# A mixture of experts on one core: the last expert's block moved into the counted loop, and the output matrices asked for by SyncE

## What is computed

```python
def moe_ffn(h, router_w, router_b, w_in, w_out):      # t: 512 tokens x 1024
    ...
    top_p, top_e = lax.top_k(in_group, TOP_K)         # 2 of 16 experts for each token
    ...
    for e in range(N_EXPERTS):
        gu = t @ w_in[e]                              # 1024 x 768
        act = jax.nn.silu(gu[:, :D_EXPERT]) * gu[:, D_EXPERT:]
        y = y + gates[:, e:e + 1] * (act @ w_out[e])  # 384 x 1024
```

## Time and profile before

| | |
|---|---|
| median of three runs | 2024.51 us (2021.44 to 2024.57) |
| the profiled execution, its own time | 2025.37 us |
| its span, first to last instruction | 2023.0 us |
| PE matmul busy, share of the span | 1597.4 us, 79% |
| DVE busy | 931.6 us, 46% |
| ACT busy | 696.4 us, 34% |
| POOL busy | 148.4 us, 7% |
| mean granted TensorE clock | 0.865 of full speed |
| bytes moved | 279.68 MB |

### The profile page before, as it was taken

The page is one execution under the profiler, slowest core; times in us unless marked ns, Lnnn a source line. Parts: engine busy times, 40 slices in busy tenths (PEclk is TensorE's granted clock), DMA queues, the critical chain, the costliest instruction groups (busy, mean ns, idle before and its releaser), DMA issues. The chain is left out here.

```text
span 2023.0 us, 19236 instructions
## 1 busy us (share of the span) xinstructions
PE 1597.4 (79%) x7495; PEld 1287.3 (64%) x7495; DVE 931.6 (46%) x1327; ACT 696.4 (34%) x1080; POOL 148.4 (7%) x162
## 2 busy tenths in 40 slices
PE   6992799376689793999973898879688793999973
PEld 5881767365577472878852787768577472878852
DVE  3224456534362525666624324552263526666623
ACT  3211234312251413555522325131251413655521
POOL 0001000100000001111010002140000001111110
PEclk8995558657899896999996899989899896999996
DMA  3324000001232026799962241213232016799963
GB/s 135 101 64 69 2 1 1 2 1 63 86 125 86 0 84 235 286 356 356 354 223 83 94 156 63 84 42 104 86 125 86 0 42 243 285 357 360 349 215 125
DMA packets 110604, 279.68 MB, mean 138 GB/s; under 512 B 40865, under 2 KB 43570, under 8 KB 105906
## 3 DMA queue, kind: packets, MB, share of 16 engines
q1 hardware_dynamic: 94962, 207.13, 29.9%
q10 hardware_dynamic: 5760, 54.53, 7.2%
q0 software_dynamic: 9792, 16.80, 2.2%
HBM read 273.11 MB, written 24.12 MB: 147 GB/s over the span
## 5 line engine op out<-in xcount | busy, mean ns | idle before, releaser
L185 DVE TENSOR_TENSOR w_lo<-w_stage,w_hi 128x2048 fp32r<-128x2048 f32 (+2 forms) x74 | 171.4, 2326 | 414.1 <-ACT w_hi L175 414.1
L175 ACT ACTIVATE w_hi<-w_stage 128x2048 fp32r<-128x2048 f32 (+2 forms) x74 | 135.9, 1847 | 473.0 <-PE bank L214 374.2
L2102 PE MATMUL bank<-e_wo,e_actT 128*128 128x512 f32 x408 | 181.0, 593 | 3.0 <-ACT e_actT L2162 3.0
L1996 DVE TENSOR_TENSOR e_wi_lo<-e_wi,w_hi 128x1536 fp32r<-128x1536 f32 x64 | 112.5, 1757 | 57.2 <-ACT w_hi L1992 57.2
L2102 PEld LDWEIGHTS bank<-e_wo,e_actT 128*128 128x128 f32 x408 | 76.7, 190 | 84.9 <-issue 83.1
L1996 DVE TENSOR_TENSOR e_wi_lo<-e_wi,w_lo 128x1536 fp32r<-128x1536 f32 x64 | 112.5, 1758 | 17.9 <-ACT w_lo L1992 17.9
L1992 ACT ACTIVATE w_hi<-e_wi 128x1536 fp32r<-128x1536 f32 x64 | 95.2, 1490 | 49.8 <-PE bank L2091 38.0
L1992 ACT ACTIVATE w_lo<-e_wi 128x1536 fp32r<-128x1536 f32 x64 | 95.0, 1484 | 18.2 <-PE bank L2091 17.1
L2090 PE MATMUL bank<-e_wi_lo,e_hx_hi 128*128 128x384 f32 x272 | 92.9, 342 | 0.0
L2091 PE MATMUL bank<-e_wi_lo,e_hx_hi 128*128 128x384 f32 x272 | 92.5, 340 | 0.0
L2218 DVE TENSOR_TENSOR e_hx_lo<-bank,e_hx_hi 128x512 fp32r<-128x512 f32 x68 | 43.8, 685 | 86.3 <-ACT e_hx_hi L2155 86.3
(11 more groups left out here) (470 smaller groups left out, 3908.7 us busy)
## 6 DMA issues: line engine op xcount, KB each, us to landing
e_wi<-in_moe_w_in SPq DMA_DIRECT2D x136, 768.0 KB, 6.0
e_wo<-in_moe_w_out ACTq DMA_DIRECT2D x32, 1536.0 KB, 9.0
w_stage<-in_x_wkv SPq DMA_DIRECT2D x16, 1024.0 KB, 5.1
w_stage<-in_sg_w_in SPq DMA_DIRECT2D x16, 1024.0 KB, 5.3
w_stage<-in_hyb_w_in SPq DMA_DIRECT2D x10, 1024.0 KB, 5.1
w_stage<-in_x_wq SPq DMA_DIRECT2D x8, 1024.0 KB, 6.2
w_stage<-in_x_wo SPq DMA_DIRECT2D x8, 1024.0 KB, 5.9
w_stage<-in_sg_w_out SPq DMA_DIRECT2D x8, 1024.0 KB, 5.0
```

The costliest lines, as they stand in the source:

```text
L175: act.activation(self.w_hi[h][:, :, :cols], self.stage[h][:, :, :cols], ACT.Copy)\
L185: dve.tensor_tensor(self.w_lo[h][:, :, :cols], self.stage[h][:, :, :cols], self.w_hi[h][:, :, :cols], ALU.subtract).then_inc(self.lo_done[ ...
L1996: dve.tensor_tensor(self.lo[q][:, :, :], self.raw[q][:, :, :], self.hi[q], ALU.subtract).then_inc(self.wi_los[q], 1)
L2102: ins = pe.matmul(y_ps[n][:, :], auT[:, f, :], wo[j][:, f, n * GC:(n + 1) * GC], start=f == 0, stop=f == CO - 1)
```

## The change

Three things change. The diff is cut to them; the rest of it moves semaphore counts by one and makes `slots` and `meta` one column larger.

1. Straight-line code now ends with block 14 (`L = NE - 1`). The loop starts with block 15, so it makes one pass more. The first entry of `meta` is expert 15, and its count is one more. In the loop a pass uses buffer 1, and turns the tokens of the next block behind its own products.
2. The output matrices of experts 2 to 14 are asked for by SP, behind the input matrix of the same expert, and wait for `wo_used`. ACT asks for none in straight-line code but the one of expert 1.
3. The tokens of block 1 are turned behind the products of block 0, no longer ahead of them.

```diff
-MAXB = (2 * S) // P + NE - 1
+MAXB = (2 * S) // P + NE
...
+                dve.memset(ebf[:, 0:1], float(NE - 1))
+                link(dve.tensor_scalar(ebf[:, OV + 1:OV + 2], cum[0:1, NE - 1:NE], 1.0, None, ALU.add))
...
             def _(sp):
-                for e in range(2, NE):
+                for e in range(2, L):
                     w.load_in(sp, e, e)
-                with sp.Fori(0, extra(sp)) as i:
+                    sp.wait_ge(wo_used, e - 1)
+                    w.load_out(sp, e, wo[e % 2])
+                with sp.Fori(0, rest(sp)) as i:
...
-                for b in range(2):
-                    pe.wait_ge(w.hx_in[b], 16)
+                def turn_tokens_of(b):
+                    pe.wait_ge(w.hx_in[b % 2], 16 * (b // 2 + 1))
                     if b:
                         pe.wait_ge(h_lo, b)
-                    turn_tokens(b)
-                for b in range(NE):
+                    turn_tokens(b % 2)
+
+                turn_tokens_of(0)
+                for b in range(L):
...
                     if b:
                         outputs_of(b - 1)
+                    else:
+                        turn_tokens_of(1)
...
-                outputs_of(NE - 1)
-                with pe.Fori(0, extra(pe)) as i:
+                outputs_of(L - 1)
+                with pe.Fori(0, rest(pe)) as i:
+                    pe.wait_ge(h_lo, i + NE)
+                    for q in range(CI):
+                        pe.wait_ge(w.wi_los[q], i + NE)
+                        product(1, q)
                     pe.wait_ge(w.hx_in[0], i * 16 + 16 * (NE // 2 + 1))
                     turn_tokens(0)
...
                     finish(b % 2)
-                    if b + 2 < NE:
-                        w.load_out(act, b + 2, wo[b % 2])
...
+                with act.Fori(0, rest(act)) as i:
                     e = expert(act, i)
-                    act.dma_start(wo[0][:, :, :], ...).then_inc(w.wo_in[0], 16)
+                    act.dma_start(wo[1][:, :, :], ...).then_inc(w.wo_in[1], 16)
+                    for q in range(CI):
+                        act.wait_ge(wi_used[q], i + L)
+                        act.wait_ge(w.wi_in[q], i * 16 + 16 * NE)
+                        act.activation(w.hi[q], w.raw[q][:, :, :], ACT.Copy).then_inc(w.wi_his[q], 1)
...
+                    silu()
                     act.wait_ge(h_turned, i + NE + 1)
-                    keep_tokens(0)
...
+                    keep_tokens(1)
```

More of the change, by code:

```diff
@@ L2060, in _ @@
                     scatter(b, b % 2, slots[:, 1, b:b + 1])
[L2061 to L2065, removed]
+                with pool.Fori(0, rest(pool)) as i:
+                    pool.tensor_copy(ix[:, 0:1], slots[:, 0, bass.ds(i + NE, 1)]).then_inc(ix_set, 1)
+                    pool.wait_ge(h_turned, i + NE)
+                    pool.wait_ge(ix_set, i * 2 + 1)
                     pool.sem_inc(passed, 1)
                     w.gather(pool, None, 0, ix[:, 0:1], h_dram)
-                    pool.wait_ge(y_act, i + NE + 1)
-                    pool.wait_ge(y_dve, i + NE + 1)
+                    pool.tensor_copy(ix[:, 1:2], slots[:, 1, bass.ds(i + L, 1)]).then_inc(ix_set, 1)
+                    pool.wait_ge(ix_set, i * 2 + 2)
+                    pool.wait_ge(y_act, i + NE)
+                    pool.wait_ge(y_dve, i + NE)
                     pool.sem_inc(passed, 1)
[L2071 to L2075, removed]
+                    scatter(None, 1, ix[:, 1:2])
+                    pool.wait_ge(w.hx_in[0], i * 16 + 16 * (NE // 2 + 1))
+                    pool.wait_ge(stored[1], i * 16 + 16 * (NE // 2))
+                    pool.sem_inc(passed, 1)
+                pool.wait_ge(stored[0], 16 * (NE // 2))
             @block.tensor
@@ L2134, in _ @@
                     turn_activations()
[L2135 to L2136 removed]
+                outputs_of(L - 1)
[4 more added lines that the diff above has]
+                        product(1, q)
                     pe.wait_ge(w.hx_in[0], i * 16 + 16 * (NE // 2 + 1))
                     turn_tokens(0)
[L2139 to L2143, removed]
[L2144 to L2149 removed]
+                    pe.wait_ge(multiplied, i + NE)
+                    turn_activations()
+                    pe.wait_ge(aT_out, i + NE)
+                    pe.wait_ge(w.wo_in[1], i * 16 + 16 * (NE // 2))
+                    pe.wait_ge(y_act, i + L)
+                    pe.wait_ge(y_dve, i + L)
+                    outputs(1)
             @block.scalar
@@ L2232, in finish_of @@
                     finish(b % 2)
[L2234 to L2238, removed]
+                dve.wait_ge(h_hi, 1)
+                keep_tokens(0)
+                for b in range(L):
+                    if b + 1 < L:
                         for q in range(CI - 1):
@@ L2251, in _ @@
                         keep_tokens(b % 2)
-                finish_of(NE - 1)
-                with dve.Fori(0, extra(dve)) as i:
-                    dve.wait_ge(h_hi, i + NE + 1)
[L2255 to L2263, removed]
+                finish_of(L - 1)
+                with dve.Fori(0, rest(dve)) as i:
+                    for q in range(CI):
+                        dve.wait_ge(w.wi_his[q], i + NE)
+                        dve.tensor_tensor(w.lo[q][:, :, :], w.raw[q][:, :, :], w.hi[q], ALU.subtract).then_inc(w.wi_los[q], 1)
+                    dve.wait_ge(silued, i + NE)
+                    multiply()
+                    dve.wait_ge(h_hi, i + NE + 1)
+                    keep_tokens(1)
+                    dve.wait_ge(wo_used, i + NE)
+                    dve.wait_ge(stored[1], i * 16 + 16 * (NE // 2 - 1))
+                    finish(1)
 def moe_combine(m, layer, w, wgt, y_dram):
```

61 lines of the change are left out of this document (30 added, 31 removed).

## The result

The changed kernel takes 2051.12 us (median of four runs, 2041.65 to 2054.64), the one before 2022.97 us in the same comparison. The ratio is 1.0138, with a 95% interval of 1.0096 to 1.0179: slower by 28 us (19 to 36 by the interval), as forecast (2054). But two of the three terms behind that number were badly wrong, and it was luck that their errors cancelled. The profiled execution took 2049.9 us against 2025.37 before.

A forecast was written before the change was run, and what follows sets the result against it. PE was taken to set the pace mid-stage, with transfers having little to spare. Start 6.2, steady part 7.2 and end 1.1 made 14.5 us a layer, 29 for two layers, so about 2054 us, ranging from 2041 to 2068.

The forecast's parts named there:

- the four stretches in the table: One layer cut at start, blocks to 14, end, and hand-over to `moe_combine`; forecast +6.2, +7.2, +1.1 and 0 us.
- The start: Block 1's tokens turned behind block 0's products: PE idle about 4.8 us, then half clock, +6.2 us a layer.
- the bounds 3.9 and 6.2: Start of the stage: +3.9 us a layer as the low end, +6.2 if the idle gap loses the clock.
- The steady part: Blocks 2 to 13: PE waits 1.2 us in every second block, six waits, +7.2 us a layer.
- The burst: SP's requests after PE's outputs: output matrix first, then four input quarters, 1536 + 4 x 768 KB.
- the chain through DVE to `multiply`: Steady part: quarter 2's high and low parts precede DVE's `multiply`, which PE needs to turn the activations.
- the slack of 11.5 us: Steady part: quarter 2 may land 11.5 us after the request before PE has to wait.
- the eight loads of `moe_combine`: Steady part: 4096 KB burst used as measure, giving 11.4 us, or 12.7 with gather and scatter.
- The end: Block 15 in the loop: two passes of about 24.6 us, +1.1 us a layer, bounds -3.5 and +3.1.
- two are 49.2, against 48.97 for block 15 in the row and one pass as it was: End of the stage: two loop passes after the change replace straight-line block 15 plus one pass before.
- The burst runs at the stage's own rate: Rival for the steady part: burst at 357 GB/s, +13.8 us a layer there, 2067 us in all; chance 0.12.
- That the change doesn't do what it says: Loop at the end: more or fewer passes than two; given no chance of its own.

The follow-up runs named there:

- alone: Kernel before with only the later turning of block 1's tokens (part 3) added: 2032.21 us, ratio 1.0060.
- beside the loop's part: Changed kernel with ACT asking for the output matrices as before, 1992.85 us, against the same with the later turning undone too, 1977.83 us.
- the spare turnings: Changed kernel plus 20 unused identity turnings on PE ahead of the turning of activations in blocks 2, 4, ..., 12: 2030.07 us, ratio 1.0045.

## Why the prediction was right, and where it was not

**The time and the sign were right, the sum was not.** Slower by 28 us was measured, 29 forecast. Of the four stretches in the table, the start held and the other three did not. Their errors are -1.1, +23.6, -25.2 and +2.7 us a layer, and it is chance that they cancel.

**The start: right.** 5.1 us in layer 0 of the profile, 6.5 a layer alone and 7.5 beside the loop's part, for 6.2. The gap (4.78 for 4.8) and the clock behind it came as worked out. By this the choice between the bounds 3.9 and 6.2 was the right one. One step in it did not come: I let the clock rise at the same moment as before and took 0.7 us off for it, but it rose 8.2 us after the first turning in the changed kernel, against 10.4 before. The products of block 0 took 10.2 us against 10.4, so nothing was lost, and that is most of the 1.1 us between 5.1 and 6.2.

**The steady part: the mechanism was right, the size four times too small.** The burst, the chain through DVE to `multiply` and the recurrence in every second block stand in the trace, and the slack of 11.5 us is about 12 there. Two steps failed. The first is the landing of quarter 2, put at 12.7 us from the eight loads of `moe_combine`; it was 14.7 in the burst shown, and the six waits of layer 0 were 3.2 us on average instead of 1.2. I had the better row and took it as the far bound: at the stage's own 357 GB/s I worked out 13.8. The burst ran at 362 GB/s, and quarter 2 came later even than that gives. In the 14.66 us to its landing 5.02 MB were moved: 0.56 for gather and scatter (I had 0.5), and 4.46 where output matrix and quarters 0 to 2 are 3.93. The other 0.53 MB were two thirds of quarter 3, which had not to be there yet; why the transfers mix so, and why two of the six waits are 4 us, was not tried. The second is the clock: I charged the half clock for gaps of 5 us and gave it no price for gaps of 1 to 3 us, although the same prediction had them in it. It cost 1.6 to 1.75 us a gap. With 3.2 for the wait that is 28.7 to 29.6, six times a layer, near the 30.8 of the table.

**The end: the premise was wrong.** The step that failed is "two are 49.2, against 48.97 for block 15 in the row and one pass as it was", with its remark that the number of passes needs no chance of its own. I read one pass before as a count of one. It was a count of zero, and so the changed kernel made one pass where I had two. A pass took 24.8 us, for 24.6 worked out, so the arithmetic of a pass held; there was one and not two, which makes the end 24.1 us shorter. The last stretch, the hand-over to `moe_combine`, which I had at nothing, is a consequence: with a real block as the last one there is something to scatter. From the start of the last scatter to the first request of `moe_combine` it was 3.9 us before (1087.73 to 1091.6), it is 6.5 in the changed kernel (1097.18 to 1103.67), and 6.0 without the loop (1047.39 to 1053.42), where the last scatter is a real one too.

**The rivals.** "The burst runs at the stage's own rate", to which I gave 0.12, was the nearest in its mechanism, with a wait of 2.3 us, still under the 3.2 measured. It would have given 2067. That the change doesn't do what it says, to which I gave nothing, is what happened at the end, to the good.

## What to carry to other kernels

Look in the trace for what a loop's pass did, not only that it ran: the bytes that its transfers moved tell a real pass from an empty one (0.22 MB against 0.00 here), and a loop whose body runs once at a count of zero needs a branch in front of it if its count is mostly zero. When a wait is put into a queue, count the bytes that must land before the next thing on the critical chain, and put that thing first; here the same wait cost about 56 us with the output matrix ahead of the quarters and nothing that shows with it behind them. Price every new gap of TensorE twice, as time and as clock.

## What the runs showed of the hardware that was not expected

The granted clock fell to 0.50 for a time behind a gap of only 2.74 us, and behind one of 2.56, while the gap that the prediction read its fall from was one of 9.85 us. The Trainium skill, "TensorE: Matmul & The Clock Gate", part 1 on the clock gate, describes activity as what keeps the clock up; the spare turnings bear this out, since with 0.54 us of the gap left the window behind it has 1.00.

Whether the output matrix stood in the same queue as the quarters or in another made no difference (2049.22 and 2051.12 us), and neither did the queue it was asked on when it came behind them (1991.30 and 1992.85). The Trainium skill, "DMA: Bandwidth & Descriptors", section on issuing engines not being separate DMA queues, says that transfers started by scalar, sync or gpsimd run on the same 16 DMA engines and interleave there, and the runs agree.
